# Fillers of the state-space passes in another order

## The chip, the cores and the metric

The kernel runs as one program on one core of a Trainium2 chip. The metric is the device time of one execution in microseconds (us): before the change 3735.56 us, the median of three runs (3731.65 to 3735.74). The engines are TensorE (PE, matmuls), VectorE (DVE), ScalarE (ACT), GpSimd (Pool) and the queue of SyncE (SP), which fetches the weights.

## The reference

A first network of two layers (SwiGLU feed-forward, a mixer of latent attention, a gated convolution and a long convolution, another feed-forward) is followed by a second of one layer. Its mixer projects the normed input into z, xBC, dt, q/k/v and gates. One branch is a Mamba-2 block:

```
xBC = silu(causal_depthwise_conv(xBC, conv_w, conv_b))
y = ssd_chunked(xs, dt, A, Bm, Cm) + d_skip * xs
y = y * silu(z)
yg = rmsnorm of y within each of 4 groups of 512 channels, times ssm_norm
y_ssm = yg @ w_ssm_out
```

The other branch is dilated attention. Then `mixed = sigmoid(gate_0) * y_ssm + sigmoid(gate_1) * y_att`, `x = x + mixed @ w_mix_out`, a SwiGLU feed-forward and a last norm. The sequence has 512 tokens, the model 1024 channels, everything in float32. The state-space scan works in 4 chunks of 128 tokens: products inside a chunk with the decay matrix (`reach`), and a state carried between chunks.

## The kernel before, in words

Activations lie transposed: channels on 128 partitions, 512 tokens along a row. All weights come as blocks of 128x1024, in the order in which PE uses them (`arrange`, `second_blocks`), by SP's queue into four `raw` buffers. Pool splits each block into a rounded high part (L427, `w_hi`) and the rest (L430, `w_lo`), two buffers of each; it starts on a block when PE has begun the block before it (`w_begun`). PE makes each product of three matmuls (L519, L523, L524), so a block of 8 tiles is 24 matmuls of 128x512.

The change lies in the second network's mixer, in `ssm_group(g)`, which exists once for PE, for ACT and for DVE and is written out for g = 0 to 3. Each pass works on one group of 512 channels (8 heads): cumulative sums of dt, turning B and x with transposes, B times C (`cb`), the states (`b_time`, `x_left`), then four pairs of heads. For each pair PE spreads the decay rows over partitions (`spread`, L956, L960), ACT takes exponentials (L1279, L1285, `reach`), DVE multiplies with `cb` (`reach_end`, L1820), PE makes the products (L980, L985), DVE adds the skip, the state part and the gate z (L1831 to L1839), ACT squares, DVE sums the squares. Behind the fourth pair PE sums them over partitions (L590), ACT takes the root (L1088), and DVE and ACT scale and split the normed y into `ssm_hi` and `ssm_lo` (`norm_scale`, L1419 to L1430).

Since this chain waits often, PE works on fillers in between, at places written out by hand in the three streams. A projection tile (`proj_tile`) is one block, 24 matmuls into one PSUM bank; an output block (`out_block`) is one block of `w_ssm_out` times the normed y of the group before, 12 matmuls into each of two banks. Both take their banks in turn from three (`FILL` = 5, 6, 7): `fill_bank` waits until the bank's last user has been copied out by DVE (`proj_free`). DVE's side of a tile: `conv_tile(k)` copies one of the six xBC tiles of the next group into `xbc_pad` (L1721), `conv_taps` applies the four taps (L1735, three times L1738), `z_tile(i)` copies a z tile, `att_gate(m)` (in the last pass, where there is no next group) a gate tile, and its `out_block` adds two banks into `ssm_sum` (L1756, L1758). `arrive(k)` is conv tile or gate tile k, `taps(k)` its taps. ACT applies SiLU to the conv tiles and the z tiles once its norm is through. DVE, PE and ACT each run strictly in the order written, so DVE must copy the tiles out in the order in which PE makes them.

Behind the norm of group 3, DVE multiplies `att_sum` by the eight sigmoids (L1868), and then the merge starts: per two channels tiles, two gate tiles and one output block of group 3.

Pool's order: `split_blocks` up to a block, then `decay_inputs(g)` (L490), which makes `x_left` from `x_time`.

Of the kernel before, what the change touches and what calls it, by code (L numbers as in the profile page):

```python
# [25 lines left out]
DC = D // P  # L26
F = 2816
FC = F // P
LAYERS = 2
# [129 lines left out]
def build(nc, io):  # L159
    ctx = ExitStack()  # L160
    with ctx:
# [253 lines left out]
        def _(pool):  # L415
# [78 lines left out]
            for g in range(SG):  # L494
                end = LAYERS * LAYER_BLOCKS + SECOND_AHEAD + (3 if g else 4) + g * GROUP_BLOCKS
                split_blocks(at, end)
                decay_inputs(g)
                at = end
# [3 lines left out]
        def _(pe):  # L502
# [389 lines left out]
            def ssm_group(g):  # L892
# [12 lines left out]
                if g:  # L905
                    out_block(4)
                else:
                    proj_tile()
                    proj_tile()
# [11 lines left out]
                if g:  # L921
                    out_block()
                else:
                    proj_tile()
# [11 lines left out]
                proj_tile()  # L936
# [11 lines left out]
                if g:  # L948
                    out_block()
                else:  # L950
                    proj_tile()
# [15 lines left out]
                for pair in range(4):  # L967
# [4 lines left out]
                    if pair in (1, 2, 3):  # L972
                        proj_tile()
                    pe.wait_ge(reach_done, c.next(reach_done, 2))
# [14 lines left out]
                if g:  # L989
                    out_block()  # L990
                else:
                    proj_tile()
                pe.wait_ge(y_taken, c.next(y_taken))
                norm_sum_matmul(4)
                for n in range(4 if g == 0 else 5 if g + 1 < SG else 3):
                    proj_tile()
# [44 lines left out]
        def _(act):  # L1041
# [154 lines left out]
            def second_mixer():  # L1196
# [67 lines left out]
                def ssm_group(g):  # L1264
# [29 lines left out]
                    else:  # L1294
                        for m in range(DC):
                            act.wait_ge(att_gate_in, c.next(att_gate_in))
                            nc.scalar.activation(gate_logits(m), gate_logits(m), ACT.Sigmoid,
                                                 bias=cols2[:, SG * GROUP_COLS + 8 + m:SG * GROUP_COLS + 9 + m]
                                                 ).then_inc(att_gate_open, 1)
# [32 lines left out]
        def _(dve):  # L1332
# [427 lines left out]
            def ssm_group(g):  # L1760
# [22 lines left out]
                if g:  # L1783
                    out_block(g - 1, 0)
                else:
                    z_tile(0)
                    z_tile(1)
# [4 lines left out]
                if g:  # L1792
                    out_block(g - 1, 1)
                else:
                    z_tile(2)
# [6 lines left out]
                arrive(0)  # L1802
# [7 lines left out]
                taps(0)  # L1810
                if g:
                    out_block(g - 1, 2)
                else:
                    z_tile(3)

# [8 lines left out]
                arrive(1)  # L1824
                taps(1)
                if g == 0:
                    dve.wait_ge(z_out, c.next(z_out, 4))
                for pair in range(4):
# [15 lines left out]
                    if pair < 3:  # L1844
                        arrive(2 + pair)
                        taps(2 + pair)
# [3 lines left out]
                if g:  # L1850
                    out_block(g - 1, 3)
                else:
                    arrive(5)
                    taps(5)
                norm_scale(4, [xs[:, i, :] for i in range(4)], at_g + G_NORM, [ssm_hi[:, i, :] for i in range(4)],
                           [ssm_lo[:, i, :] for i in range(4)], gain=cols2, out=rms2, via=scaled2)
                if g:
                    arrive(5)
                    taps(5)
                if more:  # L1860
                    for i in range(4):
                        z_tile(i)
                else:
                    att_gate(6)
                    att_gate(7)
                    for m in range(DC):
# [253 lines left out]
def second_blocks(i):  # L2120
# [8 lines left out]
    for g in range(SG):  # L2129
        ahead = group_tiles(w_x, w_b, w_c, g + 1) + z_blocks(z, g + 1) if g + 1 < SG else gates[DC:]  # L2130
        if g:
            out += [beside[0], beside[1], ahead[0], beside[2]] + ahead[1:5] + [beside[3]] + ahead[5:]
        else:
            out += beside[0:3] + [ahead[0], beside[3]] + ahead[1:]
# [99 lines left out]
```

## Time and profile before

| | |
|---|---|
| median of three runs | 3735.56 us |
| the profiled execution | 3730.05 us |
| its span, first to last instruction | 3728.3 us |
| PE busy | 3409.8 us, 91% |
| DVE busy | 1851.6 us, 50% |
| Pool busy | 1970.5 us, 53% |
| ACT busy | 766.3 us, 21% |
| HBM traffic | 76 GB/s over the span |

The profile comes from one execution. "Busy" is the time in which an engine worked on at least one instruction; PE's matmuls are pipelined and their modelled ends overlap, so distances are best read from start to start. The chain that ended last is followed backwards from the last instruction, each step to what released it. The state-space passes take from 2807 to about 3242 us of the span.

### The profile page before, as it was taken

What the parts mean: (1) busy time and instruction counts of PE and PEld (TensorE: products, weight loads), DVE (VectorE), ACT (ScalarE), POOL (GpSimd) and SP (SyncE); (2) the same over time, 40 slices, a digit from 0 to 9 for tenths busy, and PEclk for the clock granted to TensorE, in tenths of its full rate; (3) what the DMA queues carried; (4) which work ended last, traced back from release to release, by engine and by line L of the source; (5) the groups of instructions that cost most, each with busy time, mean ns of one, the idle gap of its engine ahead of it and who ended that gap; (6) DMA issues with size and microseconds to landing.
All of it is one profiled execution on the core that took longest, in us unless ns stands there. A gap on an engine that the chain in (4) does not pass through costs nothing.

```text
span 3728.3 us, 45715 instructions
## 1 busy us (share of the span) xinstructions
PE 3409.8 (91%) x14460; PEld 2636.7 (71%) x14460; DVE 1851.6 (50%) x2107; ACT 766.3 (21%) x1229; POOL 1970.5 (53%) x1148
## 2 busy tenths in 40 slices
PE   7999878889999999977888999788889899999997
PEld 6888645358887888755436888567767677778886
DVE  5331576654322432277555331465567777864313
ACT  3210101432211221110242221211112222212211
POOL 5666471136666666647004666444445455566664
PEclk9999979899999999997899999899999999999998
DMA  3333300012332233320001333221122222223332
GB/s 122 96 96 96 112 17 23 23 41 95 96 96 97 91 97 99 120 71 23 12 12 63 97 100 96 71 84 62 62 65 68 68 68 68 80 91 96 97 97 76
DMA packets 84569, 283.72 MB, mean 76 GB/s; under 512 B 9382, under 2 KB 17958, under 8 KB 83816
## 3 DMA queue, kind: packets, MB, share of 16 engines
q1 hardware_dynamic: 74016, 268.84, 22.6%
q10 hardware_dynamic: 10440, 13.41, 1.1%
q8 instruction: 66, 1.08, 0.1%
q14 instruction: 47, 0.39, 0.0%
HBM read 280.12 MB, written 2.10 MB: 76 GB/s over the span
## 4 chain that ended last, share of the span: by engine, by line
PE 75%; DVE 18%; issue 4%; ACT 2%; DMA 1%; DVEq 1%; ACTq 0%; SPq 0%
PE bank L519 21%; PE bank L524 21%; PE bank L523 21%; DVE y L1480 2%; PE bank L760 2%; PE bank L735 1%; DVE x_lo L1347 1%; PE bank L675 1%; PE bank L691 1%; DVE xbc L1738 1%; PE bank L643 1%; PE bank L749 1%; DVE scaled L1422 1%; DVE short L1467 1%; DVE ssm_lo L1430 1%
## 5 line engine op out<-in xcount | busy, mean ns | idle before, releaser
L427 POOL TENSOR_SCALAR w_hi<-raw 128x1024 fp32r<-128x1024 f32 x504 | 550.3, 1092 | 1643.9 <-PE bank L519 1637.0
L430 POOL TENSOR_TENSOR w_lo<-raw,w_hi 128x1024 fp32r<-128x1024 f32 x504 | 1269.8, 2519 | 42.1
L519 PE MATMUL bank<-x_hi,w_hi 128*128 128x512 f32 x2800 | 1121.3, 400 | 63.6 <-DVE x_lo L1347 45.4
L523 PE MATMUL bank<-x_lo,w_hi 128*128 128x512 f32 x2800 | 1102.2, 394 | 0.0
L524 PE MATMUL bank<-x_hi,w_lo 128*128 128x512 f32 x2800 | 1101.9, 394 | 0.0
L519 PEld LDWEIGHTS bank<-x_hi,w_hi 128*128 128x128 f32 x2800 | 534.1, 191 | 206.1 <-issue 74.4
L523 PEld LDWEIGHTS bank<-x_lo,w_hi 128*128 128x128 f32 x2800 | 534.8, 191 | 115.4 <-issue 6.2
L524 PEld LDWEIGHTS bank<-x_hi,w_lo 128*128 128x128 f32 x2800 | 533.2, 190 | 113.9
L519 PE MATMUL bank<-hidden_hi,w_hi 128*128 (+1 forms) x880 | 346.7, 394 | 0.0
L524 PE MATMUL bank<-hidden_hi,w_lo 128*128 (+1 forms) x880 | 345.0, 392 | 0.0
L523 PE MATMUL bank<-hidden_lo,w_hi 128*128 (+1 forms) x880 | 341.5, 388 | 0.0
L1367 DVE SCALAR_TENSOR_TENSOR x<-bank,x 128x512 f32<-128x512 f32 x64 | 44.3, 692 | 536.1 <-PE bank L524 525.4
L1388 DVE TENSOR_TENSOR up<-bank,rstd 128x512 f32<-128x512 f32 x110 | 76.2, 692 | 460.1 <-PE bank L524 456.3
L1393 DVE TENSOR_TENSOR hidden_lo<-hidden,hidden_hi 128x512 f32 x110 | 181.3, 1649 | 121.6 <-ACT hidden_hi L1069 121.6
L1067 ACT ACT_TABLE_LOAD x110 | 141.1, 1283 | 388.7 <-DVE gate L1386 388.7
L1051 ACT ACTIVATE x_hi<-x,gains 128x512 fp32r<-128x512 f32 x80 | 57.6, 720 | 668.5 <-DVE x L1367 657.6
L524 PEld LDWEIGHTS bank<-hidden_hi,w_lo 128*128 128x128 f32 x880 | 165.2, 188 | 38.7
L523 PEld LDWEIGHTS bank<-hidden_lo,w_hi 128*128 128x128 f32 x880 | 165.2, 188 | 37.0
L519 PEld LDWEIGHTS bank<-hidden_hi,w_hi 128*128 128x128 f32 x880 | 165.4, 188 | 32.9
L1069 ACT ACTIVATE hidden_hi<-hidden 128x512 f32 x110 | 69.7, 634 | 477.8 <-DVE hidden L1390 477.8
L1390 DVE TENSOR_TENSOR hidden<-gate_silu,up 128x512 f32<-128x512 f32 x110 | 105.5, 959 | 38.1 <-DVE up L1388 25.5
L1347 DVE SCALAR_TENSOR_TENSOR x_lo<-x,gains,x_hi 128x512 fp32r<-128x512 f32 x80 | 101.3, 1266 | 31.1 <-DVE x L1367 15.6
(305 smaller groups left out, 3639.2 us busy)
## 6 DMA issues: line engine op xcount, KB each, us to landing
raw<-in_w SPq DMA_DIRECT2D x504, 512.0 KB, 3.5
dft<-in_dft ACTq DMA_DIRECT2D x2, 2048.0 KB
dft<-in_dft ACTq DMA_DIRECT2D x8, 512.0 KB, 4.2
x<-in_x SPq DMA_DIRECT2D x2, 1024.0 KB, 6.6
out<-x SPq DMA_DIRECT2D x4, 512.0 KB, 2.6
mask<-in_mask ACTq DMA_DIRECT2D x1, 1536.0 KB, 6.6
decay<-in_decay ACTq DMA_DIRECT2D x2, 512.0 KB
sel<-in_sel ACTq DMA_DIRECT2D x1, 768.0 KB, 4.3
```

The lines of the kernel that those rows point to most:

```text
L427: nc.gpsimd.tensor_scalar(w_hi[:, s % 2, :], raw[:, s, :], 1.0, 0.0, ALU.mult, ALU.add).then_inc(w_rounded, 1)
L430: nc.gpsimd.tensor_tensor(w_lo[:, s % 2, :], raw[:, s, :], w_hi[:, s % 2, :].bitcast(F32), ALU.subtract).then_inc(w_split, 1)
L519: first = nc.tensor.matmul(out, hi_w, hi, start=start, stop=False)
L523: nc.tensor.matmul(out, hi_w, lo, start=False, stop=False)
L524: return nc.tensor.matmul(out, lo_w, hi, start=False, stop=stop)
L760: last = nc.tensor.matmul(bank[7][0:V_DIM, :], mla_v[:, kt, h * V_DIM:(h + 1) * V_DIM], probs_t[:, kt % 2, :], start=kt == 0, stop=kt == T ...
L1067: nc.scalar.activation(gate_silu[:], gate[:], ACT.Silu).then_inc(gate_activated, 1)
L1347: link(nc.vector.scalar_tensor_tensor(x_lo[:, m, :], x[:, m, :], g, x_hi[:, m, :].bitcast(F32), ALU.mult, ALU.subtract), x_split)
L1388: link(nc.vector.tensor_tensor(up[:], bank[2 * b + 1][:], rstd[:], ALU.mult), pair_free)
L1390: link(nc.vector.tensor_tensor(hidden[:], gate_silu[:], up[:], ALU.mult), hidden_ready)
L1393: link(nc.vector.tensor_tensor(at(hidden_lo), hidden[:], at(hidden_hi).bitcast(F32), ALU.subtract), hidden_split)
L1480: link(nc.vector.scalar_tensor_tensor(acc, src, w, acc, ALU.mult, ALU.add))
```

## The change

The fillers of the passes change places in PE's stream, DVE's stream and the order of the weight blocks; their number is the same.

- PE, group 1 to 3, before: output blocks behind the sums, behind `cb`, before the pairs and behind pair 3; tiles behind the turned x, behind `spread(0)`, in pairs 1, 2 and 3, and five (in group 3 three) behind the norm. After: tiles behind the sums and behind `cb`; output blocks behind the turned x, before the pairs and in pairs 0 and 1; tiles behind `spread(0)`, in pairs 2 and 3, behind pair 3, and four (in group 3 two) behind the norm.
- PE, group 0 (no output blocks): one tile each behind sums and `cb`, two behind the turned x, two before the pairs, one behind `spread(0)`, none in pairs 0 and 1, one in pairs 2 and 3 each, one behind them, four behind the norm.
- DVE: conv tiles 0 and 1 come at the head, 2 ahead of the pairs, 3, 4 and 5 around and behind the norm's scaling; z tiles 0 and 1 (group 3: gate tiles 6 and 7) in pairs 2 and 3; output blocks behind the turned x, behind the states and in pairs 0 and 1.
- The eight gates of group 3 go through ACT and DVE in the order 0, 1, 2, 6, 7, 3, 4, 5.
- Pool makes `x_left` of group 0 after three blocks instead of four.

```
--- before.py
+++ after.py
@@ -492,7 +492,7 @@
                                             ).then_inc(x_decayed, 1)
 
             for g in range(SG):
-                end = LAYERS * LAYER_BLOCKS + SECOND_AHEAD + (3 if g else 4) + g * GROUP_BLOCKS
+                end = LAYERS * LAYER_BLOCKS + SECOND_AHEAD + 3 + g * GROUP_BLOCKS
                 split_blocks(at, end)
                 decay_inputs(g)
                 at = end
@@ -902,11 +902,7 @@
                     last = nc.tensor.matmul(bank[1][0:SH, ch * P:(ch + 1) * P], dt_time[:, 1, ch, own], tri_on,
                                             start=True, stop=True)
                 last.then_inc(rows_ready, 1)
-                if g:
-                    out_block(4)
-                else:
-                    proj_tile()
-                    proj_tile()
+                proj_tile()
 
                 pe.wait_ge(conv_out, c.next(conv_out, 2))
                 for ch in range(CH):
@@ -918,10 +914,7 @@
                     last = nc.tensor.matmul(bank[3][:, rows], xs[:, 4, rows], xs[:, 5, rows],
                                             start=True, stop=True)
                 last.then_inc(cb_ready, 1)
-                if g:
-                    out_block()
-                else:
-                    proj_tile()
+                proj_tile()
 
                 pe.wait_ge(gap_ready, c.next(gap_ready))
                 pe.wait_ge(rows_split, c.next(rows_split))
@@ -933,7 +926,11 @@
                         last = nc.tensor.transpose(bank[ch % 2][:, i * P:(i + 1) * P],
                                                    xs[:, i, ch * P:(ch + 1) * P], ident[:])
                     last.then_inc(x_turned, 1)
-                proj_tile()
+                if g:
+                    out_block(4)
+                else:
+                    proj_tile()
+                    proj_tile()
 
                 pe.wait_ge(b_timed, c.next(b_timed))
                 pe.wait_ge(cb_masked, c.next(cb_masked))
@@ -949,6 +946,7 @@
                     out_block()
                 else:
                     proj_tile()
+                    proj_tile()
 
                 def spread(pair):
 
@@ -969,8 +967,10 @@
                     pe.wait_ge(pair_decay, c.next(pair_decay))
                     if pair + 1 < 4:
                         spread(pair + 1)
-                    if pair in (1, 2, 3):
+                    if pair >= 2:
                         proj_tile()
+                    elif g:
+                        out_block()
                     pe.wait_ge(reach_done, c.next(reach_done, 2))
                     if pair:
                         pe.wait_ge(y_taken, c.next(y_taken))
@@ -986,13 +986,10 @@
                                                 state[:, ch - 1, pair * P:(pair + 1) * P],
                                                 xs[:, 5, ch * P:(ch + 1) * P], start=True, stop=True)
                     last.then_inc(y_parts, 1)
-                if g:
-                    out_block()
-                else:
-                    proj_tile()
+                proj_tile()
                 pe.wait_ge(y_taken, c.next(y_taken))
                 norm_sum_matmul(4)
-                for n in range(4 if g == 0 else 5 if g + 1 < SG else 3):
+                for n in range(4 if g + 1 < SG else 2):
                     proj_tile()
 
             def second_mixer():
@@ -1292,7 +1289,7 @@
                         conv_silu(g + 1)
                         z_silu()
                     else:
-                        for m in range(DC):
+                        for m in (0, 1, 2, 6, 7, 3, 4, 5):
                             act.wait_ge(att_gate_in, c.next(att_gate_in))
                             nc.scalar.activation(gate_logits(m), gate_logits(m), ACT.Sigmoid,
                                                  bias=cols2[:, SG * GROUP_COLS + 8 + m:SG * GROUP_COLS + 9 + m]
@@ -1780,26 +1777,24 @@
                 dve.wait_ge(rows_rounded, c.next(rows_rounded))
                 link(nc.vector.tensor_tensor(a_rows[32:32 + SH, :], bank[1][0:SH, :], a_rows[0:SH, :].bitcast(F32),
                                              ALU.subtract), rows_split)
-                if g:
-                    out_block(g - 1, 0)
-                else:
-                    z_tile(0)
-                    z_tile(1)
+                arrive(0)
+                taps(0)
                 dve.wait_ge(cb_ready, c.next(cb_ready))
                 link(nc.vector.tensor_tensor(cb[:].rearrange("p (c l) -> p c l", c=CH),
                                              bank[3][:].rearrange("p (c l) -> p c l", c=CH),
                                              tri[:, 0:P].unsqueeze(1).broadcast_to([P, CH, P]), ALU.mult), cb_masked)
-                if g:
-                    out_block(g - 1, 1)
-                else:
-                    z_tile(2)
+                arrive(1)
                 dve.wait_ge(left_ready, c.next(left_ready, 2))
                 for ch in range(CH):
                     dve.wait_ge(x_turned, c.next(x_turned))
                     nc.vector.tensor_tensor(heads(x_time[:, ch, :]), heads(bank[ch % 2][:]),
                                             wide(dt_time[:, 0, ch, g * SH:(g + 1) * SH]), ALU.mult
                                             ).then_inc(x_timed, c.add(x_timed))
-                arrive(0)
+                if g:
+                    out_block(g - 1, 0)
+                else:
+                    z_tile(0)
+                    z_tile(1)
                 dve.wait_ge(state_in, c.next(state_in, CH - 1))
                 link(nc.vector.tensor_copy(state[:, 0, :], bank[2][:]))
                 for ch in range(1, CH - 1):
@@ -1807,11 +1802,12 @@
                                                  wide(a_whole[:, ch, :]), ALU.mult))
                     link(nc.vector.tensor_tensor(state[:, ch, :], state[:, ch, :], bank[2 + ch][:], ALU.add),
                          state_done if ch == CH - 2 else dve_step)
-                taps(0)
                 if g:
-                    out_block(g - 1, 2)
+                    out_block(g - 1, 1)
                 else:
+                    z_tile(2)
                     z_tile(3)
+                taps(1)
 
                 def reach_end(pair):
                     for b in range(2):
@@ -1821,8 +1817,7 @@
                                                 ).then_inc(reach_done, c.add(reach_done))
 
                 reach_end(0)
-                arrive(1)
-                taps(1)
+                arrive(2)
                 if g == 0:
                     dve.wait_ge(z_out, c.next(z_out, 4))
                 for pair in range(4):
@@ -1841,29 +1836,32 @@
                         dve.wait_ge(norm_squared, c.next(norm_squared, 2 if pair == 2 else 1))
                         link(nc.vector.tensor_tensor(square_sum[:], square[:, 0, :] if pair == 2 else square_sum[:],
                                                      square[:, pair - 1, :], ALU.add))
-                    if pair < 3:
-                        arrive(2 + pair)
-                        taps(2 + pair)
+                    if pair < 2:
+                        if g:
+                            out_block(g - 1, 2 + pair)
+                        if pair == 0:
+                            taps(2)
+                    elif more:
+                        z_tile(pair - 2)
+                    else:
+                        att_gate(4 + pair)
                 dve.wait_ge(norm_squared, c.next(norm_squared))
                 link(nc.vector.tensor_tensor(square_sum[:], square_sum[:], square[:, 3, :], ALU.add))
                 dve.sem_inc(norm_summed, 1)
-                if g:
-                    out_block(g - 1, 3)
+                arrive(3)
+                norm_scale(4, [xs[:, i, :] for i in range(4)], at_g + G_NORM, [ssm_hi[:, i, :] for i in range(4)],
+                           [ssm_lo[:, i, :] for i in range(4)], gain=cols2, out=rms2, via=scaled2)
+                taps(3)
+                arrive(4)
+                taps(4)
+                if more:
+                    z_tile(2)
+                    arrive(5)
+                    taps(5)
+                    z_tile(3)
                 else:
                     arrive(5)
-                    taps(5)
-                norm_scale(4, [xs[:, i, :] for i in range(4)], at_g + G_NORM, [ssm_hi[:, i, :] for i in range(4)],
-                           [ssm_lo[:, i, :] for i in range(4)], gain=cols2, out=rms2, via=scaled2)
-                if g:
-                    arrive(5)
-                    taps(5)
-                if more:
-                    for i in range(4):
-                        z_tile(i)
-                else:
-                    att_gate(6)
-                    att_gate(7)
-                    for m in range(DC):
+                    for m in (0, 1, 2, 6, 7, 3, 4, 5):
                         dve.wait_ge(att_gate_open, c.next(att_gate_open))
                         link(nc.vector.tensor_tensor(att_sum[:, m, :], att_sum[:, m, :], gate_logits(m), ALU.mult))
 
@@ -2128,10 +2126,10 @@
     beside = z_blocks(z, 0)
     for g in range(SG):
         ahead = group_tiles(w_x, w_b, w_c, g + 1) + z_blocks(z, g + 1) if g + 1 < SG else gates[DC:]
-        if g:
-            out += [beside[0], beside[1], ahead[0], beside[2]] + ahead[1:5] + [beside[3]] + ahead[5:]
-        else:
-            out += beside[0:3] + [ahead[0], beside[3]] + ahead[1:]
+        tail = ahead[6:]
+        out += ahead[0:2] + (beside[0:2] if g else beside) + [ahead[2]]
+        out += [beside[2], beside[3]] if g else []
+        out += tail[0:2] + ahead[3:5] + tail[2:3] + ahead[5:6] + tail[3:]
         beside = group_out(i["w_ssm_out_2"][0], g)
     for n in range(4):
         out += gates[2 * n:2 * n + 2] + [beside[n]]
```

## Rows read from the trace of the kernel before

**Rows 1.** The page: busy time of the engines, and the chain that ended last.

```profile
PE 3409.8 (91%) x14460; PEld 2636.7 (71%) x14460; DVE 1851.6 (50%) x2107; ACT 766.3 (21%) x1229; POOL 1970.5 (53%) x1148
...
PE 75%; DVE 18%; issue 4%; ACT 2%; DMA 1%; DVEq 1%; ACTq 0%; SPq 0%
```

**Rows 2.** Timeline of PE (start, length, engine, line): pass starts, first gate block's second half.

```profile
2807.09 0.30 PE L899 MATMUL bank<-dt_time,tri 128*128 128x32 f32 x2
...
2920.41 0.30 PE L899 MATMUL bank<-dt_time,tri 128*128 128x32 f32 x2
...
3030.78 0.30 PE L899 MATMUL bank<-dt_time,tri 128*128 128x32 f32 x2
...
3139.20 0.30 PE L899 MATMUL bank<-dt_time,tri 128*128 128x32 f32 x2
...
3245.24 0.50 PE L519 MATMUL bank<-ssm_hi,w_hi 128*128 128x512 f32 x1
```

**Rows 3.** Waits of PE, 2800 to 3265 us: total, times, longest.

```profile
PE bank L590 <- DVEq L1849: 11.8, 4, 4.6
PE bank L956 <- ACT reach L1285: 9.0, 8, 2.2
PE bank L519 <- ACT reach L1285: 7.3, 4, 2.0
```

**Rows 4.** Stretches: length, busy PE, PEld, DVE, ACT, POOL, granted clock, DMA, GB/s.

```profile
2850.00:2858.00 8.00, 4.97 (x35) 3.80 (x35) 6.29 (x10) 4.82 (x18) 0.00 (x0) 1.00 0.18 66
...
2895.00:2899.50 4.50, 4.50 (x9) 2.89 (x10) 4.32 (x6) 0.79 (x2) 1.95 (x2) 0.50 0.01 4
...
3093.00:3098.00 5.00, 5.00 (x16) 3.92 (x16) 4.93 (x6) 0.00 (x0) 3.82 (x2) 0.66 0.00 0
```

**Rows 5.** Timeline of PE, group 1: the tile ahead of pair 0, spread, products.

```profile
2952.41 0.39 PE L519 MATMUL bank<-x_hi,w_hi 128*128 128x512 f32 x1
...
2957.87 0.39 PE L956 MATMUL bank<-a_rows,sel_hi 128*128 128x512 f32 x1
...
2959.09 1.09 PE L980 MATMUL bank<-reach,x_time 128*64 128x128 f32 x16
```

**Rows 6.** Timeline of DVE, group 0, one `conv_taps`.

```profile
2864.11 0.55 DVE L1735 TENSOR_SCALAR xbc<-xbc_pad,cols 128x512 f32<-128x512 f32 x1
2864.69 2.33 DVE L1738 SCALAR_TENSOR_TENSOR xbc<-xbc_pad,cols,xbc 128x512 f32<-128x512 f32 x3
```

**Rows 7.** Timelines of PE and DVE, group 3, products of pair 3 to the gates.

```profile
3205.22 1.09 PE L980 MATMUL bank<-reach,x_time 128*64 128x128 f32 x16
...
3206.93 0.48 PE L519 MATMUL bank<-ssm_hi,w_hi 128*128 128x512 f32 x1
...
3213.55 1.10 PE L590 MATMUL bank<-square_sum,ones 128*128 128x512 f32 x2 [0.78 <-DVEq L1849]
...
3230.48 0.69 DVE L1721 TENSOR_TENSOR xbc<-bank,rstd 128x512 f32<-128x512 f32 x1
...
3232.99 9.20 DVE L1868 TENSOR_TENSOR att_sum<-att_sum,xbc 128x512 f32<-128x512 f32 x6
...
3244.49 1.53 DVE L1721 TENSOR_TENSOR gate_a<-bank,rstd 128x512 f32<-128x512 f32 x2
```

**Rows 8.** Timeline of three engines, group 3, between pairs 1 and 2.

```profile
3190.43 0.39 PE L519 MATMUL bank<-x_hi,w_hi 128*128 128x512 f32 x1
...
3192.42 2.70 POOL L430 TENSOR_TENSOR w_lo<-raw,w_hi 128x1024 fp32r<-128x1024 f32 x1
...
3192.80 2.74 DVE L1836 TENSOR_TENSOR xbc<-xbc,scaled 128x384 f32<-128x384 f32 x1
...
3195.57 0.69 DVE L1839 TENSOR_TENSOR xbc<-xbc,z_act 128x512 f32<-128x512 f32 x1
```

**Rows 9.** Timeline of ACT, group 0, square and exponentials of a pair.

```profile
2873.88 0.63 ACT L1258 ACTIVATE square<-xbc 128x512 f32<-128x512 f32 x1 [7.40 <-DVE xbc L1839]
...
2874.89 2.17 ACT L1285 ACTIVATE reach<-bank,a_own 128x128 f32<-128x128 f32 x8
```

## The prediction, as it was made before the result

> **What bounds the kernel now.** I read the page first, then the waits of the tensor engine (PE) in the state-space stage, then its clock, then the order of time. The page [rows 1] gives PE 91% of the span and three quarters of the chain that ended last; VectorE (DVE) holds 18%. So a microsecond counts only where PE stands still. The change touches one stretch of about 440 us, the four group passes, which start at 2807.1, 2920.4, 3030.8 and 3139.2; the first output block behind them starts its second half at 3245.24 [rows 2]. The periods are 113.3, 110.4 and 108.4 us, and the last pass is 106.0 us to that half block. Every pass sends the same 14 weight blocks through PE, before and after, so only the idle time and the clock can differ.
>
> The waits [rows 3]: 11.8 us over four for the last sum before the group norm, 9.0 and 7.3 us for the exponentials of `reach` ahead of and inside the pairs. Behind the longest, 4.6 us before the norm of group 0, PE ran at half its clock: granted 0.50 of 2.4 GHz for 4.5 us, so half of that, 2.2 us, was lost; group 1 repeats it. After the wait of 2.2 us ahead of the pairs the clock stayed at 1.00, but in group 2 it fell to 0.66 for 5 us after one of under 2 [rows 4]. What the change aims at is thus about 28 us of waits and some 6 us of slow clock.
>
> **The change part by part.** T is a projection tile, O an output block, each one weight block, 5.46 us from start to start [rows 5]; O takes 5.6.
>
> Head. T T O O replace O O T O before the last T; same count, so a pass still reaches its pair 0 after 37.5 us (2920.41 to 2957.87, [rows 2, 5]). The copies have the same place ahead of the turned x (a tile's copy instead of a block's). New on DVE is `taps(0)` here, 2.9 us [rows 6], beside PE's T. It fits, except where DVE arrives late from the pass before; I take 0.7 us for that in groups 1 to 3 (bounds 0 and 2), and 1.6 in group 0, where DVE is still in the taps of tile 5 when the pass starts. Pool's `decay_inputs` after three blocks instead of four in group 0 follows the fourth block, which now stands ahead of the states: 0 to 0.5 us.
>
> Pair 0 gets a cover (groups 1 to 3): spread 1.2, O 5.6, products 1.7 [rows 5, 7]. The first instruction behind the products is at 37.5 + 8.5 = 46.0. The wait there, about 0.9 us, goes. Late next is not ACT but a bank.
>
> Pair 1, the step I find decisive. O needs two of the three fill banks. The second half of O in pair 1 needs the bank of the first half of O in pair 0, and DVE empties that only at the end of pair 0: behind the skip, the product, `reach_end(1)`, the add, the gate (L1839). Those start when the products end; between them and that half block PE has only the spread (1.2) and half a block (2.8). When does L1839 end? In [rows 8] the pass has the same arrangement (spread straight behind the products): the tile starts at 3190.43, L1839 ends at 3196.26, 5.8 us later, because L1836 (384 columns, so less than the 0.69 of L1839 when alone) waits for Pool's `w_lo`, started by that same tile. With the copy 6.4. Stall 6.4 - 2.8 = 3.6 us; if no conflict fell there it would be 0.9. I take 3.6, since every pass of before has one such blocked instruction per pair. Next boundary 46.0 + 1.2 + 5.6 + 3.6 + 1.7 = 58.1.
>
> The Trainium skill (SBUF — State Buffer, Who interferes with whom) says that a DVE instruction with two SBUF inputs and a GpSimd instruction that reads SBUF shut each other out for the whole instruction. The trace agrees: 2.74 us beside `w_lo`, and the wait ends with it. By the rule a copy from PSUM is not held, as above.
>
> Pairs 2 and 3. ACT's exponentials of pair 3 wait for the gate of pair 1 and take 3.2 us with the square [rows 9]. That gate ends at 58.1 + 1.2 + 5.7 = 65.0, so the tile of pair 3 starts at 68.2 where PE is ready at 66.5: 1.7 us, as in the trace of before (7.3 us over four passes). Products end at 68.2 + 5.5 + 1.7 = 75.4.
>
> Norm. Conv tiles leave the pairs (0.7 + 2.9 us each), so DVE enters pair 3 in time. Behind the start of the tile that follows pair 3 the fourth pass of before, which has no taps, needed 6.6 us to the norm's matmul (3206.93 to 3213.55, [rows 7]); now there is a `z_tile` (0.7) as well: 7.3. The tile covers 5.6, so 1.7 us stay in each pass, 6.8 of 11.8 in all, and more in group 3 than its 0.78. Norm at 82.7, and the slow clock behind it goes.
>
> Behind the norm. This is the bill for moving a tile ahead of it: four tiles stay, and the bank of the fourth is that of the first. That one (`arrive(4)`) is emptied behind `norm_scale` and now `taps(3)`. `norm_scale` ends 16.9 us after the norm's matmul (3213.55 to 3230.48, [rows 7]); with taps 2.9 and the copy 0.7 it is 20.6, and PE is ready at 0.5 + 3 x 5.46 = 16.9. Stall 3.7 us in groups 0 to 2 (bounds 0, if nothing were blocked in `norm_scale`, and 5, if a tap is blocked too). Pass end 82.7 + 20.6 + 5.5 = 108.8, with the head 109.5: against 110.4 a gain of 0.9, against 108.4 a loss of 1.1.
>
> Group 3. Between the norm and the second half of the first gate block there were three tiles, two gate tiles and half a block, 31.7 us, and DVE emptied the first gate tile (3244.49 + 0.7) exactly then, behind 11.5 us of products with `att_sum` [rows 7]. Two tiles are left now; DVE saves one copy and needs 30.8 us after the norm, while PE is there after 26. So the half block starts at 82.7 + 0.7 + 30.8 = 114.2 against 106.0: 8.2 us later. The order (0, 1, 2, 6, 7, 3, 4, 5) follows arrival and costs nothing, as the gates are ready ahead of the products.
>
> Group 0. Gone: 2.2 us (ACT had waited for z tile 3 ahead of pair 0, now it comes a tile earlier), 2.9 of the norm wait and 2.2 of clock. New: 1.6 at the head, 3.7 behind the norm; pairs 0 and 1 lose their cover, where about 1.2 us more is waited. Net -1.
>
> Sum: -1.0 - 0.9 + 1.1 + 8.2 = +7.4 us at full clock. The seven new stalls of 3.6 to 5 us each (three at pair 1, three behind the norm, one at the gates) lie between the 2.2 us that left the clock alone and the 4.5 that halved it. Bounds 0 and 7 x 2.2 = 15; stalls behind which DVE is late anyway hide part. I take 5. Together +12: the profiled execution, 3730.05 us (span 3728.3), would be 3742; the median of before is 3735.56, so the predicted time is 3747.5.
>
> **Rivals.**
> A, the forecast: covers traded for bank stalls; +5 to +20.
>
> B, faster: L1836, L1839 and the norm's instructions miss `w_lo`, since Pool's splits move with the blocks. It decides at pair 1: if L1839 ends within 2.7 us of the tile's start. With all conflicts gone a pass is 46.0 + 9.5 + 15.6 + 5.6 + 22 = 99 us, and the sum some -30; half of it, -14, gives 3722. For it: PE's long norm waits surely shrink. Against: [rows 8] and its like in every pass.
>
> C, a wash: stalls of 2 instead of 3.6 us at pair 1 and behind the norm (6 x 1.6 = 10 us less), clock kept: 7.4 - 10 = about -2, 3733. For it: the wait of 2.2 us with full clock behind it.
>
> D, clearly slower: the clock falls behind every stall, and the head's lateness is 2 us: 7.4 + 15 + 4 = +26, 3762. For it: [rows 4]. The Trainium skill (TensorE: Matmul & The Clock Gate, HAM oscillation) describes kernels that pay for the slow clock again in each turn of waiting and burst; the trace shows it twice here in four passes.
>
> **How the numbers follow.** A change under about 0.2% (7.5 us) can't be told from none. A 0.50 (of this 0.04 below +7.5), B 0.18, C 0.20, D 0.12. Slower 0.46 + 0.12 = 0.58; within 0.04 + 0.20 = 0.24; faster 0.18. For eight in ten I leave out most of B and the end of D: 3727 to 3761.
>
> **What would show it.** In the profile of after: a wait of PE for the copy of `ssm_sum` in the middle of the output block of pair 1, 3 to 4 us, in groups 1 to 3; a wait for `xbc_pad` ahead of the fourth tile behind the norm; one of 4 to 5 us for `gate_a` in the first gate block; norm waits of 1 to 2 us at full clock; passes of about 112, 110 and 110 us. It is wrong if L1839 of pair 0 ends before half of that block is through, or if DVE is not what PE waits for behind the norm.

## The result, and the profile after

The changed kernel takes 3757.9 us (median of 4 runs, 3750.65 to 3760.71), the kernel before 3735.0 (4 runs, 3731.65 to 3735.74). The ratio is 1.0061, interval [1.0048, 1.0074]: 22.9 us slower. The forecast was +12, inside a range of 3727 to 3761.

The page of the changed kernel: busy time of the engines, and the shares of the chain that ended last.

```profile
PE 3418.9 (91%) x14460; PEld 2644.5 (70%) x14460; DVE 1872.4 (50%) x2107; ACT 764.7 (20%) x1229; POOL 1970.6 (52%) x1148
...
PE 73%; DVE 20%; issue 4%; ACT 2%; DMA 1%; DVEq 1%; ACTq 0%; SPq 0%
```

Against [rows 1] the instruction counts are the same, PE is 9 us busier for the same matmuls, and 2% of the chain moved from PE to DVE. (The second profile of the changed kernel, `again` below, has PE at 3409.5 us: the whole program's busy time moves by that much from execution to execution, so only sums over a stretch are used from here on.) Where in time? One stretch for each pass of the changed kernel, the last one up to the second half of the first output block of the merge (columns as in [rows 4]; behind them the same of the kernel before):

```profile
2816.30:2931.79 115.49, 104.10 (x493) 82.77 (x492) 84.44 (x93) 30.61 (x65) 55.22 (x31) 0.94 0.22 69
2931.79:3044.51 112.72, 101.56 (x494) 79.90 (x493) 89.73 (x93) 27.09 (x62) 55.86 (x31) 0.97 0.21 66
3044.51:3157.78 113.27, 102.05 (x494) 80.16 (x492) 88.75 (x92) 27.08 (x62) 56.20 (x31) 0.97 0.21 63
3157.78:3273.64 115.86, 103.37 (x506) 81.00 (x504) 82.57 (x80) 29.06 (x65) 58.85 (x33) 0.99 0.22 70
```

```profile
2807.09:2920.41 113.32, 101.21 (x493) 79.49 (x492) 87.54 (x95) 32.74 (x69) 55.87 (x31) 0.97 0.20 65
2920.41:3030.78 110.37, 101.37 (x493) 79.83 (x492) 81.76 (x92) 27.38 (x62) 54.76 (x31) 0.97 0.21 68
3030.78:3139.20 108.42, 101.07 (x494) 79.27 (x492) 83.97 (x92) 27.37 (x62) 56.12 (x31) 0.98 0.21 68
3139.20:3245.24 106.04, 101.86 (x506) 80.19 (x504) 76.01 (x76) 27.42 (x61) 57.84 (x33) 1.00 0.24 75
```

The first two numbers of a row, length and PE's busy time, are enough. The passes take 457.3 us instead of 438.1, so +19.2. PE's busy time grew by 5.6 (411.1 against 405.5) for the same matmuls: that is slow clock. Its idle time grew by the other 13.6. From the half block to PE's last matmul it is 471.1 against 469.5, +1.6, the clock again. Together 20.8 us. The first pass also starts 9.2 us later, though nothing ahead of it differs; the first experiment settles what that is.

PE's waits of the changed kernel, 2800 to 3290 us (line numbers have shifted: L1718 is the copy of a tile, before L1721; L1753 and L1755 take an output block, before L1756 and L1758; L954 is `spread`, before L956; L926 turns x, before L933; L1831 and L1834 end a pair's chain, before L1836 and L1839):

```profile
PE bank L519 <- DVE xbc_pad L1718: 9.5, 3, 3.2
PE bank L519 <- DVE ssm_sum L1755: 7.3, 2, 3.7
PE bank L590 <- DVEq L1850: 7.0, 4, 1.9
PE bank L926 <- DVE x_time L1790: 5.3, 4, 2.5
PE bank L519 <- ACT reach L1282: 5.0, 3, 1.7
PE bank L519 <- DVE gate_a L1718: 4.4, 1, 4.4
PE bank L519 <- DVE ssm_sum L1753: 3.7, 1, 3.7
PE bank L954 <- ACT reach L1282: 3.1, 2, 2.4
```

Compare [rows 3]: the norm wait fell from 11.8 to 7.0 (forecast 6.8), the waits for `reach` from 16.3 to 8.1. Three kinds are new, all waits for a bank: 11.0 us at pair 1 (three times 3.7), 9.5 behind the norm (three times 3.2), 4.4 at the gates. The wait for `x_time`, the turned x, grew too: 5.3 in all, longest 2.5 in group 0, where the kernel before has 3.0 and 0.9. The place of the first new stall, on DVE and Pool in group 1 (start, length, engine, line), against [rows 8]:

```profile
2979.52 2.14 DVE L1816 TENSOR_TENSOR reach<-reach,trig 128x512 f32<-128x512 f32 x2
2981.58 2.70 DVE L1831 TENSOR_TENSOR xbc<-xbc,scaled 128x384 f32<-128x384 f32 x1
2984.32 0.69 DVE L1834 TENSOR_TENSOR xbc<-xbc,z_act 128x512 f32<-128x512 f32 x1
2985.04 1.42 DVE L1753 COPY ssm_sum<-bank 128x512 f32<-128x512 f32 x2
```

```profile
2981.20 2.67 POOL L430 TENSOR_TENSOR w_lo<-raw,w_hi 128x1024 fp32r<-128x1024 f32 x1
```

```profile
2985.79 0.50 PE L519 MATMUL bank<-ssm_hi,w_hi 128*128 128x512 f32 x1 [3.68 <-DVE ssm_sum L1753]
```

Read it downwards: Pool begins `w_lo` at 2981.20, the small product begins 0.4 us later and ends 0.4 us after Pool, then gate, first copy, and PE goes on at 2985.79. And the granted clock (the number ahead of the last two) behind the seven new stalls, in order of time, with two stretches of group 0 ahead of them, behind a wait of 2.5 us for the turned x and one of 2.4 us for `reach`:

```profile
2833.60:2838.60 5.00, 4.96 (x19) 4.32 (x20) 1.96 (x3) 0.00 (x0) 4.78 (x5) 0.66 0.00 0
2878.00:2886.00 8.00, 8.00 (x29) 6.26 (x28) 3.13 (x6) 3.17 (x10) 3.94 (x2) 0.79 0.07 10
2923.40:2932.00 8.60, 8.52 (x27) 6.81 (x27) 8.17 (x10) 0.63 (x1) 3.91 (x2) 0.65 0.22 61
2985.80:2991.00 5.20, 5.20 (x36) 4.17 (x37) 3.62 (x6) 2.42 (x9) 0.00 (x0) 1.00 0.23 91
3036.30:3044.50 8.20, 8.19 (x24) 6.53 (x25) 7.84 (x8) 0.63 (x1) 3.91 (x2) 0.65 0.21 64
3098.50:3104.00 5.50, 5.49 (x28) 4.06 (x28) 3.48 (x5) 2.44 (x9) 0.00 (x0) 0.69 0.21 84
3150.50:3157.80 7.30, 7.23 (x25) 5.78 (x26) 6.94 (x8) 0.63 (x1) 4.21 (x2) 0.77 0.12 27
3211.60:3217.80 6.20, 6.20 (x33) 4.62 (x34) 0.65 (x1) 2.42 (x9) 0.00 (x0) 0.72 0.16 66
3273.60:3278.30 4.70, 4.66 (x13) 3.68 (x14) 1.38 (x2) 0.72 (x1) 0.00 (x0) 0.64 0.08 33
```

Behind six of the seven new stalls PE came back at a mean of 0.64 to 0.77 of 2.4 GHz, a mix of its two levels; behind one of 3.7 us (the third row) it kept the full clock. The first two rows show a slow clock behind shorter waits as well.

### The profile page after: what moved, and what is told of

Read it like the earlier page. It is cut to its first block, busy times and chain, and to the rows that moved or that the text cites. A ratio compares the mean times of both kernels' runs of the same rounds, so it can differ in the third digit from the quotient of the medians.

```text
span 3758.2 us, 45707 instructions
## 1 busy us (share of the span) xinstructions
PE 3418.9 (91%) x14460; PEld 2644.5 (70%) x14460; DVE 1872.4 (50%) x2107; ACT 764.7 (20%) x1229; POOL 1970.6 (52%) x1148
## 4 chain that ended last, share of the span: by engine, by line
PE 73%; DVE 20%; issue 4%; ACT 2%; DMA 1%; DVEq 1%; ACTq 0%; SPq 0%
PE bank L519 21%; PE bank L524 20%; PE bank L523 20%; DVE y L1477 2%; PE bank L760 2%; PE bank L735 1%; DVE x_lo L1344 1%; DVE xbc L1735 1%; PE bank L675 1%; PE bank L691 1%; DVE scaled L1419 1%; PE bank L643 1%; DVE ssm_lo L1427 1%; PE bank L749 1%; DVE short L1464 1%
```

## The experiments

"Passes" is the time from the first pass's start to the half block, as above: 438.1 us before, 457.3 after.

**The same two kernels again: `again` (changed), `before_again`.** No edit.

> The changed kernel once more, unaltered. In its first profile the four passes took 19.2 us longer than before (457.3 against 438.2 us), but their start was already 9.2 us late, in code that the change doesn't touch. Theory: the early 9 us are an accident of that execution (weights late, clock), so a second profile starts the passes near 2807 to 2811 us, and the passes again take 19 to 20 us more. Rival: something of the change acts on the whole program; then the passes start at about 2816 again and the whole is again +23 us.

Median 3757.4 us, ratio 1.0066 [1.0050, 1.0083]. Passes 457.4, each within 0.1 us of the first profile; the first pass starts at 2811.3 instead of 2816.3.

> The kernel before, unaltered. In the ten profiles so far the first pass starts between 2804 and 2818 us though nothing ahead of it differs, while the length of the four passes repeated to 0.1 us in two profiles of the changed kernel. If the spread is an accident of the execution, this profile has the four passes at 437.6 to 438.6 us and the start anywhere in 2804 to 2818. If the start belongs to the kernel, it is again 2807 within 1 us.

Passes 438.1, periods 113.3, 110.4 and 108.4 once more; start at 2803.6, not the 2807.1 of the first profile, and just under the band named. So the start is an accident of the execution (2803.6 to 2818.3 over 13 profiles with the same code ahead), and the length of the passes belongs to the kernel, slow clock included. From here on that length is what is compared.

**`swap`: output blocks of groups 1 to 3 in pairs 0 and 2 instead of 0 and 1.** This gives the bank of pair 0 a tile more of time. PE's part of the edit (DVE's stream and the order of the weight blocks follow it):

```
-                    if pair >= 2:
+                    if g and pair in (0, 2):
+                        out_block()
+                    elif pair >= (1 if g else 2):
                         proj_tile()
-                    elif g:
-                        out_block()
```

> Output block of pair 1 and tile of pair 2 change places in groups 1 to 3, so no block needs a bank that is emptied at the end of pair 0. Theory (bank stall): the three waits of 3.7 us and the slow clock behind two of them (1.3 us each and more) go; instead PE waits 1.7 us for the exponentials of pair 2, as it does for those of pair 3. Passes 1 to 3 get 2 to 4 us shorter each, the whole 6 to 10 us shorter than the changed kernel. Rival (DVE is the limit, a stall is only moved): the passes stay within 1 us each, the wait turns up at pairs 2 and 3 or before the norm.

Median 3747.8 us, ratio 1.0031 [1.0017, 1.0046]; passes 448.7, 8.7 less. The waits for `ssm_sum` fall from 11.0 us to 0.2; 5 us come back as waits for `reach` ahead of pairs, 1.6 to 1.7 in each pass. The sum is as my theory expected; the single passes are 2.9, 1.3 and 4.6 us shorter, where 2 to 4 each was named. Behind the half block 1.1 us come back.

**`gates`: the first two gate tiles copied between the products with `att_sum`.** The first goes ahead of all eight products, the second behind the fourth; the merge then leaves these two out (that part is not shown).

```
                     for m in (0, 1, 2, 6, 7, 3, 4, 5):
+                        if m in (0, 7):
+                            gate_tile(m // 7)
                         dve.wait_ge(att_gate_open, c.next(att_gate_open))
```

> In group 3 DVE copies the first gate tile ahead of the eight products with att_sum and the second after four of them. Theory: PE's wait of 4.44 us inside the first output block of the merge goes, and the slow clock behind it (1.6 us): 5 to 6 us shorter than the changed kernel, passes 0 to 2 unchanged. Rival: the merge is bound by DVE anyway, and the wait comes again at the second output block: under 2 us gained.

Median 3750.0 us, ratio 1.0050 [1.0033, 1.0067]. The last pass falls from 115.9 to 111.4, the rest from 471.1 to 469.7: the stall of 4.4 is gone, and with it the slow clock behind it: 5.9 us, as expected.

**`swap_gates`: both edits.**

> The changed kernel with both repairs that helped: output block and tile of pairs 1 and 2 exchanged, and the first gate tiles copied ahead of the products with att_sum. The two lie in different places, so their gains add: 8.7 and 4.5 us (6 with the clock) of the 19 to 21, leaving the stall behind the norm in groups 0 to 2. 13 to 15 us faster than the changed kernel, still 6 to 10 us slower than before. Rival (DVE the limit everywhere): under 10 us.

Median 3741.3 us, ratio 1.0012 [1.0002, 1.0021]; passes 444.1, 13.3 less, where 8.7 and 4.5 make 13.2. The two add up, also in the last pass, which both touch: 115.9 us in the changed kernel, 111.3 and 111.4 with one edit, 106.7 with both. What is left over the kernel before is 6.0 us in the passes, with the stall behind the norm (9.5 us) untouched.

**`early`: conv tile 4 copied in the middle of `norm_scale`.** It should take the stall behind the norm away.

```
+                    if midway and i == 1:
+                        midway()
...
                taps(3)
-                arrive(4)
                 taps(4)
```

> DVE copies tile 4 (arrive(4)) between the second and third split of the norm instead of behind the norm and the taps of tile 3. Theory: the wait of 3.15 us ahead of the fourth tile behind the norm goes in groups 0 to 2, and with it the slow clock of that tile (2.7, 2.6 and 1.6 us); about 1 us comes back at the start of the next pass, since z tile 2 is freed late. Each of passes 0 to 2 3.5 to 5 us shorter, the whole 11 to 15 us shorter than the changed kernel. Rival (DVE's queue behind the norm is the limit): the same stall appears one tile later, ahead of the first tile of the next pass, and the whole gains under 4 us.

A miss, for 11 to 15 us less were expected: 3761.8 us, ratio 1.0082 [1.0066, 1.0099]; passes 460.2, 2.8 more, so the rival was right. The two longest of PE's waits in `early`, then one set of taps there (group 1) with the Pool instruction beside it, and the same set in the changed kernel with Pool's next instruction:

```profile
PE bank L926 <- DVE x_time L1792: 8.3, 4, 2.5
PE bank L519 <- DVE z_act L1720: 8.1, 3, 2.7
```

```profile
3029.25 5.00 DVE L1737 SCALAR_TENSOR_TENSOR xbc<-xbc_pad,cols,xbc 128x512 f32<-128x512 f32 x3
3030.21 2.71 POOL L430 TENSOR_TENSOR w_lo<-raw,w_hi 128x1024 fp32r<-128x1024 f32 x1
```

```profile
3033.20 2.33 DVE L1735 SCALAR_TENSOR_TENSOR xbc<-xbc_pad,cols,xbc 128x512 f32<-128x512 f32 x3
3037.30 1.22 POOL L427 TENSOR_SCALAR w_hi<-raw 128x1024 fp32r<-128x1024 f32 x1 [5.27 <-PE bank L519]
```

The first pass gets 6.2 us shorter, but the stall moves on to the first tile of the next pass and to the turned x, and the other three get 2 to 4 us longer each. In the changed kernel these taps ran in 2.33 us while PE stood (3.15 us, until 3036.31) and Pool with it: Pool begins a split only when PE begins a block. With PE running, Pool's `w_lo` falls beside the taps, and they take 5.00. So a stall that is closed this way gives DVE more to do.

**`before_short` and `after_short`: hardly any `w_lo` in the passes.** Both kernels, with the low part of the weights made for 8 of 1024 columns in the blocks of the four passes (the rest of that low part is left out).

```
+                n_lo = 8 if short[0] else BLOCK * P
-                nc.gpsimd.tensor_tensor(w_lo[:, s % 2, :], raw[:, s, :], w_hi[:, s % 2, :].bitcast(F32),
+                nc.gpsimd.tensor_tensor(w_lo[:, s % 2, 0:n_lo], raw[:, s, 0:n_lo],
+                                        w_hi[:, s % 2, 0:n_lo].bitcast(F32), ALU.subtract).then_inc(w_split, 1)
```

> The kernel before, with Pool's w_lo instruction cut to 8 of 1024 columns for the weight blocks of the four passes (from the output it leaves out the low part of those weights); PE, DVE and ACT do the same work. Theory (DVE held by Pool's w_lo): DVE's chains lose their blocked instructions, 2 to 2.8 us each; the waits for exponentials and most of the norm waits go, and the clock stays up. Passes to the half block of the merge 412 to 422 us instead of 438. Rival (DVE's own length and the order decide): within 5 us of 438.

> The same cut of Pool's w_lo in the changed kernel (low part of those weights left out of the result). Theory: the stall in pair 1 falls from 3.7 to about 0.9 us, the one behind the norm (3.15) and the one in the merge (4.4) to under 1, the slow clock behind them goes; passes 408 to 422 us instead of 457, and the difference to the kernel before with the same cut is under 5 us instead of 19. Rival (the order of the banks costs the time, whatever Pool does): the difference between the two cut kernels stays 12 us or more.

3709.5 and 3703.8 us; passes 411.8 and 406.9. One execution each. So Pool's `w_lo` costs the old order 26.3 us and the new one 50.4, and without it the new order is the better by 4.9 us. PE's waits of `before_short` (all of them), then all but two of `after_short` (the others: 3.0 for `x_time`, 0.5 for `reach`):

```profile
PE bank L599 <- DVEq L1858: 6.8, 3, 2.3
PE bank L965 <- ACT reach L1294: 4.0, 5, 0.9
PE bank L942 <- DVE x_time L1808: 3.0, 4, 0.9
PE bank L528 <- ACT reach L1294: 1.1, 3, 0.4
```

```profile
PE bank L963 <- ACT reach L1291: 3.3, 2, 2.4
...
PE bank L528 <- DVE ssm_sum L1764: 3.0, 2, 1.5
PE bank L528 <- DVE ssm_sum L1762: 1.5, 1, 1.5
```

In `after_short` the norm's wait and the stall behind it are gone; the bank stall of pair 1 is 1.5 us where 0.9 was expected. In `before_short` one expectation failed: most of the norm's wait was to go, but 6.8 of 11.8 us stay; the waits for `reach` fell from 16.3 to 5.1.

**`one_short`: a single block of that kind.** The changed kernel; only the block that Pool splits while PE works on pair 1's output block, in groups 1 to 3 (the rest of its low part is left out).

```
+                if g:
+                    split_blocks(at, at + 4)
+                    short[0] = True
+                    split_blocks(at + 4, at + 5)
+                    short[0] = False
+                    at += 5
```

> The changed kernel; in groups 1 to 3 one single block, the tile that follows pair 1's output block, has its low part made for 8 of 1024 columns (the rest of that low part is left out); Pool makes it while PE works on pair 1's output block, which is when VectorE's 384-column product of pair 0 took 2.70 us. My theory (the bank stall of pair 1 comes from that one conflict): the product takes 0.5 to 0.7 us, the wait of the output block's second half on ssm_sum falls from 3.7 us to 0.5 to 1.6 in each of three passes, and the four passes fall from 457.4 us to 446 to 450. Rival (VectorE is late there for its own work): the wait stays at 3 us or more and the passes at 455 to 458. Second rival (the time comes back later in the pass as a longer wait behind the norm): the wait of pair 1 goes and the passes fall by under 4 us.

One run, 3746.8 us; passes 447.4, 10.0 less than 457.4. Pool's and DVE's rows at the same place, and then PE's waits:

```profile
2977.89 0.52 POOL L433 TENSOR_TENSOR w_lo<-raw,w_hi 128x8 fp32r<-128x8 f32 x1
```

```profile
2978.27 0.55 DVE L1840 TENSOR_TENSOR xbc<-xbc,scaled 128x384 f32<-128x384 f32 x1
```

```profile
PE bank L528 <- DVE xbc_pad L1727: 9.5, 3, 3.2
...
PE bank L528 <- DVE ssm_sum L1764: 3.0, 2, 1.5
PE bank L528 <- DVE ssm_sum L1762: 1.5, 1, 1.5
```

The product takes 0.55 us instead of 2.70, and the wait of pair 1 is 1.5 in each pass; the one behind the norm is as it was. Of the 10.0 us, 6.5 are waits of pair 1 and 4.2 are PE's busy time (406.9 against 411.1), so slow clock that followed them; the two overshoot by 0.7, which came back elsewhere.

**`late_taps`: the old order with DVE relieved ahead of the norm.** The kernel before, PE untouched; the taps of conv tiles 4 and 5 stand behind the norm's scaling, behind z tiles 0 and 1. (Tile 4's come from pair 2; tile 5's stood ahead of the scaling in group 0 alone, in groups 1 and 2 behind it but ahead of the z tiles.)

```
                     if pair < 3:
                         arrive(2 + pair)
+                    if pair < 2:
                         taps(2 + pair)
...
                     arrive(5)
-                    taps(5)
...
                 if g:
                     arrive(5)
+                if more:
+                    z_tile(0)
+                    z_tile(1)
+                    taps(4)
                     taps(5)
-                if more:
-                    for i in range(4):
-                        z_tile(i)
+                    z_tile(2)
+                    z_tile(3)
```

> The kernel before with one thing of the change's idea alone: the taps of conv tiles 4 and 5 move behind the norm's scaling, PE's order stays. Theory: DVE enters pair 3 2.9 to 5.6 us earlier, the norm waits of 4.6 and 4.5 us fall to about 1 and the slow clock behind them goes, while five tiles still cover DVE behind the norm: 8 to 13 us faster than before. Rival (DVE's work behind the norm is the limit, as the run with the early copy suggested): the taps that moved come back as waits of 2 to 3 us at the start of the next pass, within 4 us of the kernel before.

A little more than expected: median 3720.7 us (5 runs) against 3734.3, ratio 0.9961 [0.9947, 0.9975]: 13.6 us faster than the kernel before, so it beats both. Passes 426.0; the norm's waits are 3.6 instead of 11.8 us, and the clock stays up:

```profile
2814.17:2921.61 107.44, 99.03 (x494) 78.14 (x492) 84.59 (x89) 29.86 (x64) 55.22 (x31) 1.00 0.23 69
2921.61:3029.43 107.82, 99.40 (x494) 78.13 (x493) 91.77 (x97) 27.49 (x63) 55.53 (x31) 1.00 0.24 69
3029.43:3134.19 104.76, 99.10 (x493) 78.21 (x492) 88.74 (x93) 26.96 (x62) 55.33 (x31) 1.00 0.22 71
3134.19:3240.16 105.97, 101.83 (x506) 80.19 (x504) 79.93 (x79) 29.43 (x65) 57.82 (x33) 1.00 0.25 75
```

**`late_z`: the same with z tile 2 between the two sets of taps.** It takes aim at the one new wait of `late_taps`, 2.77 us at 2928.87.

> The version with the old order on PE and the taps of conv tiles 4 and 5 behind the norm's scaling, now with z tile 2 copied between the two sets of taps instead of behind both. That version had one new wait, PE on the copy of z tile 1 or 2 behind the norm, 2.8 us in one pass and little in the others. My theory: the wait goes, the taps of tile 5 end no later, 2 to 3 us less: passes 423 to 425 us against 426.0, median 3716 to 3720. Rival: PE only waits a tile later for the next copy, the passes stay within 1 us of 426 and the time at 3720 to 3722. In no case is it slower than the kernel before.

The wait went, the gain did not come: 3724.0 us (6 runs), ratio 0.9971 [0.9958, 0.9983]; passes 426.8. The rival's length of the passes holds, not its 3720 to 3722 us and not its reason: PE waits only 0.7 us more somewhere else. Group 2's tile of pair 3, first in `late_taps`, then in `late_z`, at its start on PE's timeline:

```profile
3091.38 0.50 PE L519 MATMUL bank<-x_hi,w_hi 128*128 128x512 f32 x1 [1.95 <-ACT reach L1285]
```

```profile
3089.38 0.58 PE L519 MATMUL bank<-x_hi,w_hi 128*128 128x512 f32 x1 [1.95 <-ACT reach L1285]
```

And the stretches of that tile, in the same order:

```profile
3091.40:3097.10 5.70, 5.70 (x26) 4.46 (x28) 5.60 (x7) 0.00 (x0) 3.85 (x2) 1.00 0.00 0
```

```profile
3089.40:3096.60 7.20, 7.20 (x24) 5.54 (x24) 6.95 (x8) 0.63 (x1) 3.77 (x2) 0.76 0.18 47
```

The same wait, 61.95 and 61.97 us into the pass, behind the same three shorter waits of 0.7 to 1.0 us; once at full clock and once at 0.76. The kernel before shows the same within one execution: its waits at this place are 1.96 us in group 1 and 1.93 in group 2, and only behind the second does the clock fall, to the 0.66 of [rows 4]. `late_z` lost 1.6 us in that way in groups 1 and 2 each (PE busy 100.9 and 100.7 against 99.4 and 99.1), more than the 2.8 us wait saved.

## Why the prediction was right, and where it was too small

The direction, all three new stalls and their places were right. The passes came out at 115.5, 112.7 and 113.3 us where about 112, 110 and 110 were named. For the sizes the passes of `late_taps` serve as a ruler, since the granted clock is 1.00 in all four: PE is busy for 399.4 us in them. It is good to about 1 us a pass: `before_short` has passes at clock 1.00 in which PE is busy about 1 us less (98.05 and 98.30 against 99.03 and 99.10). What a pass has above that is slow clock: 2.2, 2.0, 2.0 and 0 before (together 6.2; the forecast had "some 6"), 5.1, 2.2, 2.9 and 1.5 after (11.7).

- **Passes at full clock: the sum right, in part by luck.** Forecast 112.3, 109.5, 109.5 and 114.2, together 445.5 us (for group 0 the 113.3 of before less 1.0). Measured without the slow part: 110.4, 110.6, 110.3 and 114.3, together 445.6. Group 0 was put 1.9 us too long, groups 1 and 2 1.1 and 0.8 too short, and the errors cancel.
- **Head.** Forecast 0.7 us late in groups 1 to 3, 1.6 in group 0. The wait for the turned x there is 0.95 us (group 1) and 2.46 (group 0), but the kernel before already waits 0.71 and 0.90 for it. New are 0.2 and 1.6: group 0 right, groups 1 to 3 half a microsecond too much each.
- **Pair 1, bank stall.** Forecast 3.6 us by the conflict with `w_lo`, 0.9 without; measured 3.7 and, with that one `w_lo` cut, 1.5. `one_short` shows that conflict to be the cause of 2.2 of 3.7 us, the order of fillers of the rest; `swap` removes all of it.
- **Pair 3 and norm.** 1.7 and 1.7 us forecast, 1.66 and 1.69 measured in group 1.
- **Behind the norm.** Forecast 3.7 us, measured 3.15. That "if nothing were blocked" it would be 0 was right too: `after_short` has no such wait.
- **Gates.** The half block forecast 8.2 us later, 114.2 into the last pass; measured 115.9, of which 1.5 is clock.
- **The clock: the term that was mis-sized.** The step took 5 us from bounds of 0 and 15, on the ground that stalls of 3.6 us lie between a wait that left the clock alone and one that halved it. The clock fell behind six of the seven, and besides in group 0 behind the waits of 2.5 us for the turned x and 2.4 us for `reach`, which the step didn't count. Measured: 11.7 us in the passes and 1.6 behind the half block, 13.3 in all, 8.3 more than taken. With it the forecast of +12.4 becomes +20.7; the two profiles have +20.8. The remaining 2 us to the medians' 22.9 lie within the scatter of the start.

The +22.9 us lie above the +5 to +20 that the forecast gave its own case A and nearer to rival D's +26 than to +12. Rival D had the clock right and the head wrong (2 us more each in groups 1 to 3; it was 0.3 or less). Rival B, "faster if the conflicts miss", is what `after_short` shows: its condition was stated rightly and not met. The sum of its -30 was near too (406.9 is 31 under 438.1; four passes of its 99 us would make more, and they were 103.7, 100.1, 100.1 and 103.0), but it had not asked what the old order gains by the same: 26.

The Trainium skill (SBUF — State Buffer, Who interferes with whom) says that the one who comes first holds the shared port for its whole instruction and that the order of issue decides who is blocked. The trace agrees: Pool's `w_lo` began 0.38 us ahead of the product, kept its 2.67, and the product ended 0.41 after it.

What stays open is what decides the clock behind a wait of about 2 us: `late_taps` and `late_z` differ in it with the same wait and the same waits ahead in that pass, and so do groups 1 and 2 of the kernel before. It repeats from run to run of one kernel (`again`, `before_again`), so it is not chance; which property of the work further ahead decides was not tried. The Trainium skill (TensorE: Matmul & The Clock Gate, A second HAM failure mode: psum-queue depth-cycling) tells of a kernel that loses clock to many short idle times between groups of matmuls instead of one long one. The falls behind waits of 1.95 us may be of that sort, but no run here tests that explanation.

## What to carry to other kernels

Moving a filler ahead of a wait moves it away from another place, and with three banks in turn the bill comes where the same bank is asked for again: for each filler moved, follow its bank to the next user and ask when the in-order engine empties it. If the old order waits because the vector engine is late, give that engine less to do ahead of the wait (`late_taps`, two sets of taps moved, -13.6 us) before moving the tensor engine's work. And price each new stall of some 3 us with the slow clock behind it as the likely case (here six of seven, 1.5 to 3 us each), not as a third of the upper bound.

## What the runs showed of the hardware that was not expected

- How much a conflict between GpSimd and VectorE costs hangs on whether TensorE runs, as GpSimd's splits start with its blocks. Three taps took 2.33 us beside a standing TensorE and 5.00 beside a running one.
- With hardly any `w_lo` in four passes of 14 blocks each both orders gain, 26.3 and 50.4 us. A schedule's worth changed sign with it: +19.2 us with, -4.9 without (the short runs are one execution each).
- The same wait of 1.95 us was followed by a granted clock of 1.00 in one kernel and 0.76 in another, with the same waits before it in the pass. The slow clock repeats with the kernel to 0.1 us in a pass.
